# S5 products sent one by one inside the projection tiles of a two-layer trunk

## The chip, the core and the metric

The kernel runs on one core of one Trainium2 chip. Its engines are TensorE (PE in the profile, with its weight loads on a row of their own, PEld), VectorE (DVE), ScalarE (ACT), GpSimd (POOL) and SyncE (SP); the last two mostly issue DMAs here. The metric is the device time of one execution in microseconds (us). "Before" is the kernel without the change, "after" the one with it.

## The reference

```python
for l in range(DEPTH):                                  # DEPTH = 2, SEQ = 256, D_MODEL = 2048
    h = rmsnorm(x, g_pre_mix[l]) * (1.0 + sc1) + sh1
    y = hybrid_mixer(h, positions, w_in[l], w_out[l], ...)
    x = x + gt1 * rmsnorm(y, g_post_mix[l])
    h = rmsnorm(x, g_pre_ffn[l]) * (1.0 + sc2) + sh2
    y = conv_ffn(h, f_w_up[l], f_conv_w[l], f_conv_b[l], f_w_down[l])
    x = x + gt2 * rmsnorm(y, g_post_ffn[l])
...
def hybrid_mixer(...):
    proj = (h @ w_in)
    m_qk, m_v, m_o, m_i, m_f, s_u, n_q, n_kv, n_g = split(proj)
    y_m = mlstm_group(...)                              # 4 heads
    y_s = s5_group(s_u, ...)                            # 32 groups of 16 channels, 64 complex states each
    y_n = nsa_group(...)                                # 8 query heads, attention in "items"
    return concatenate([y_m, y_s, y_n]) @ w_out
...
def s5_group(u, ...):
    x = u @ B                                           # complex: real and imaginary part
    h[t] = a * h[t-1] + x[t]                            # scan over the sequence
    y = gelu(real(C @ h) + d_skip * u)
    return y * sigmoid(y @ w_glu + b_glu)
```

## The kernel before, in words

Everything is float32; a weight chunk of the big products is split into a high part (w_hi, by ScalarE, L1427) and a rest (w_lo, by VectorE, L2015), and TensorE adds three products. The stage of the change is the input projection of each layer: 41 column tiles n = 0 to 40 of 128 columns. A tile (`proj`, L789) takes two weight chunks, one for each half of the 2048 rows; a half is 8 row tiles of 3 matmuls of 256 columns (L798), so a tile is 48 matmuls. In layer 0 the first 12 tiles are made elsewhere, so the loop starts at n = 12.

Between the tiles TensorE gets the other work of the mixer, placed by tile number. For S5 these are blocks of 8 matmuls of 64 (or 63) columns: four input blocks (`s5_in`, L973, h = 0, 1 and part = real, imaginary) behind the tiles 18 to 21, and six output blocks (`s5_out`, L988 and L991) behind the tiles 22, 23, 24, 25, 26 and 26 (`OUT_AT`). Before its first matmul a block waits for its weight chunk (`raw_full`); the first input block also for the S5 tokens, the blocks of h = 1 for VectorE's read of the blocks of h = 0 (`s5_bv`), output blocks with part 1 for the end of the scan (`s5_h`). The last matmul of a block gives the chunk's place free (`raw_used`).

All weight chunks, of 512 KB each, go through one ring of five places in SBUF, in an order fixed beforehand (`_ring_places`): S5's chunk for tile n stands behind the second chunk of tile n+1. SyncE issues the loads in that order and waits at each until the chunk five places earlier has been split (`raw_free`, from VectorE) or used (`raw_used`, from TensorE). S5's own chunks were written to DRAM earlier in the same layer (s_in_w, s_own_w, s_out_w). A split part has four places, so ScalarE may split chunk c+4 once TensorE has used chunk c (`w_used`).

ScalarE and VectorE also work through fixed lists, tile by tile. ScalarE at tile n: split the first chunk of tile n+2 (`w_head(2n+4)`), evict tile n (`in_tile`; L1598 to L1600, L1586), split the second chunk, then the rest of that tile's work. Part of it is `s5_gelu(h)` (16 activations, L1713), which stands at the tile `OUT_AT[3h+2]` and waits for the last output block of h. From tile 27 on (`ITEM_TILE`) attention items run: at n = 27 ScalarE copies the transposed values (L1859) and then does `exps(0)` (L1724); TensorE's `scores(1)`, behind tile 28, waits for the end of `exps(0)` (`ns_e`). VectorE at tile n: `w_rest(2n+4)`, `w_rest(2n+5)` (L2015, w_lo), then for n = 19 to 24 a third of the S5 scan, then slices of the conditioning product (ada, L2021).

```python
CMP_TILE, IN_TILE, OUT_TILE, GLU_TILE, MB_TILE = 10, 18, 22, 32, 35
OUT_AT = [OUT_TILE + i for i in (0, 1, 2, 3, 4, 4)]
...
def scores(n):
    if n: ns_e.wait(pe, l, n)
```

Of the kernel before, what the change touches and what calls it, by code (L numbers as in the profile page):

```python
# [24 lines left out]
P = 128  # L25
# [8 lines left out]
UT = S_GROUPS * S_GROUP // P  # L34
# [3 lines left out]
SN = SEQ // SL  # L38
SH = ST // 2
# [20 lines left out]
KH = KT // 2  # L60
# [50 lines left out]
R_CMP, R_IN, R_OUT, R_GLU = 0, N_CMP, N_CMP + 4, N_CMP + 10  # L111
NRAW = R_GLU + 2
CMP_TILE, IN_TILE, OUT_TILE, GLU_TILE, MB_TILE = 10, 18, 22, 32, 35
OUT_AT = [OUT_TILE + i for i in (0, 1, 2, 3, 4, 4)]
BLOCKS_AT = (HT, CMP_TILE - 3)
CMP_AT = ([HT + 2 + i // 2 for i in range(N_CMP)], [CMP_TILE + i for i in range(N_CMP)])

# [88 lines left out]
def trunk(nc, x, c_cols, pos, consts, aux_d, ada_d, ada_b, glu_d, stream, out):  # L206
    with ExitStack() as ctx:
# [7 lines left out]
        at = nc.sbuf_base - 2 * KT * SEQ * 4  # L215
# [51 lines left out]
        ps = ctx.enter_context(nc.psum_tensor("ps", [P, 8, 512], F32))  # L267
# [32 lines left out]
        def sem(name):  # L300
# [8 lines left out]
        w_used = sem("w_used")  # L309
# [19 lines left out]
        raw_used = Signal("raw_used", NRAW)  # L329
# [24 lines left out]
        s5_u, s5_ut = Signal("s5_u", 1), sem("s5_ut")  # L354
# [3 lines left out]
        s5_tr, s5_tr_ev = Signal("s5_tr", UT), Signal("s5_tr_ev", UT)  # L358
# [3 lines left out]
        s5_bv, s5_h, s5_g = Signal("s5_bv", 2), Signal("s5_h", 2), Signal("s5_g", 2)  # L362
# [6 lines left out]
        ch_g, cc_mm, cc_ev = Signal("ch_g", 2), Signal("cc_mm", 1), Signal("cc_ev", 2)  # L369
# [23 lines left out]
        s5_u2, s5_cos, s5_sin, s5_dec = (  # L393
            S5T[:, 4 * i:4 * i + 4, :].rearrange("p a b -> p (a b)").rearrange("p (j n) -> p j n", j=ST) for i in range(4))
# [25 lines left out]
        s5_v = [[pair(t) for t in (28, 30, 32, 34)], [pair(t) for t in (36, 38, 0, 2)]]  # L420
# [62 lines left out]
        def raw(l, n):  # L483
            if l == 0 and n < CMP_HELD:
                return held((W_S5 + 4, W_S5 + 8, W_S5 + 12, KT // 2, 3 * KT // 4)[n])
            return ring[:, RING_RAW[l][n] % RING, :]
# [252 lines left out]
        def _(pe):  # L739
            def raw_full(l, n):  # L740

                if l == 0 and n < CMP_HELD:
                    pe.wait_ge(cmp_full, 16 * CMP_HELD)
                    return
                pe.wait_ge(ring_full[RING_RAW[l][n] % RING], ring_count(l, RING_RAW[l][n]))
# [40 lines left out]
                m.then_inc(w_used, 2)  # L786
                h_lo.wait(pe, l, 8 * n + 8)

            def proj(l, c, bank):  # L789

                for half in range(2):
                    split_ready(l * NS + c + half)
                    s = (c + half) % SPLIT
                    for kk in range(KH):
                        k = half * KH + kk
                        ks = slice(kk * P, (kk + 1) * P)
                        for p, (w, h) in enumerate(((w_hi, hT_hi), (w_hi, hT_lo), (w_lo, hT_hi))):
                            m = pe.matmul(ps[:, bank, 0:SEQ], w[:, s, ks], h[:, k, :],  # L798
                                          start=k == 0 and p == 0, stop=k == KT - 1 and p == 2)
                    m.then_inc(w_used, 1)  # L800

            def to_tokens(n, x0, c, k, summed=None):

# [75 lines left out]
            for l in range(DEPTH):  # L879
# [80 lines left out]
                                              u[:, :, :, SL - 1 - k], start=True, stop=True)  # L960
                    m.then_inc(s5_ut, 1)

                def s5_in(h, part):

                    n = R_IN + 2 * h + part
                    raw_full(l, n)
                    if h == 0 and part == 0:
                        s5_tr_ev.wait(pe, l, UT)
                        s5_u.wait(pe, l, 1)
                    if h == 1:  # L970
                        s5_bv.wait(pe, l, 1)
                    for j in range(SH):
                        m = pe.matmul(ps[:, 2 + part, j * SN:(j + 1) * SN], raw(l, n)[:, j * P:(j + 1) * P],  # L973
                                      s5_u2[:, SH * h + j, :], start=True, stop=True)
                    raw_used.by(m)

                def s5_out(h, part):

                    n = R_OUT + 3 * h + part
                    raw_full(l, n)  # L980
                    if part == 1:
                        s5_h.wait(pe, l, h + 1)
                    if h == 0 and part == 0:
                        ch_g.wait(pe, l, 2)
                    for j in range(SH):
                        js = slice(j * P, (j + 1) * P)
                        if part == 0:
                            m = pe.matmul(ps[:, 6 - h, j * SN:(j + 1) * SN], raw(l, n)[:, js], s5_u2[:, SH * h + j, :],  # L988
                                          start=j == 0, stop=False)
                        else:  # L990
                            m = pe.matmul(ps[:, 6 - h, j * SN + 1:(j + 1) * SN], raw(l, n)[:, js],  # L991
                                          s5_v[h][part - 1][:, j * SN:(j + 1) * SN - 1], start=False,
                                          stop=part == 2 and j == SH - 1)
                    raw_used.by(m)

                def compress(i):

# [160 lines left out]
                for n in range(0 if l else HT, NT):  # L1158
                    if l == 0 and n < HT + 2:
                        in_ev.wait(pe, l, 2 * (n - HT) + 2)  # L1160
                        h_lo.wait(pe, l, 8)
                    elif n >= 2:
                        if N_QK <= n - 2 < N_V:
                            qk_cv.wait(pe, l, n - 2 - N_QK + 1)
                        else:
                            in_ev.wait(pe, l, n - 1)
                    if n == 0:
                        first_tiles(l, 0, 0)
                    elif n >= 2:
                        proj(l, 2 * n, n % 2)  # L1170
                    if l and n == 1:
                        s5_b_transposes()
                    if l and n - 2 in S5_B:
                        s5_in_weights(S5_B.index(n - 2))
                    if l and n - 3 in S5_B:
                        s5_own_weights(S5_B.index(n - 3))
                    if l == 0 and n == HT + 1:
                        s5_tokens()
                    if l == 0 and n - 3 in LATE_C:
                        s5_own_weights(len(HEAD_OWN) + LATE_C.index(n - 3))  # L1180
                    for i in range(N_CMP):
                        if n == CMP_AT[l][i] + 1 and i % 4 == 3:
                            compress_sum(i // 4)
                    for i in range(N_CMP):
                        if n == CMP_AT[l][i]:
                            compress(i)
                    if n == N_G + 2:
                        gate_columns()
                    if IN_TILE <= n < IN_TILE + 4:
                        s5_in(*divmod(n - IN_TILE, 2))  # L1190
                    if n == CMP_TILE + N_CMP + 2:
                        compressed()
                    for i in range(6):
                        if n == OUT_AT[i]:
                            s5_out(*divmod(i, 3))
                    if n == ITEM_TILE - 2:
                        v_tokens(0)
                    if n == ITEM_TILE:
                        v_tokens(1)
                    if 0 <= n - ITEM_TILE < NI:  # L1200
                        scores(n - ITEM_TILE)
                    if 0 <= n - ITEM_TILE - 1 < NI:
                        weights_t(n - ITEM_TILE - 1)
                    if 0 <= n - ITEM_TILE - 2 < NI:
                        weighted_sum(n - ITEM_TILE - 2)
                    if GLU_TILE <= n < GLU_TILE + 2:
                        glu(n - GLU_TILE)
                    if n == MB_TILE:
                        glu_z.wait(pe, l, 4)
                        gate_turned(0)  # L1210
                        mg_d.wait(pe, l, 2)
                        for ck in range(2):
                            pe.transpose(ps[:, 7, 4 * ck:4 * ck + 4], rows(3, ck * P, (ck + 1) * P), K("ident", 0, 4, 4))
                        m_row.wait(pe, l, 1)
                        for ck in range(2):
                            m = pe.transpose(ps[:, 7, 8 + 4 * ck:12 + 4 * ck], rows(0, ck * P, (ck + 1) * P), K("ident", 0, 4, 4))
                        mb_mm.by(m)
                    if n == NT - 2:
                        select(2, 6, 0)
                    if n == NT - 1:  # L1220
                        mc_a.wait(pe, l, 2)
                        ns_e.wait(pe, l, NI)
                        m_scores(3, 0)
                        m_s.by(m_last[0])
                    if n == NT - 3:
                        m_tokens(0)
                    if n == NT - 2:
                        m_tokens(1)
# [1641 lines left out]
```

## Time and profile before

| | us |
|---|---|
| median of 3 runs (2419.27 to 2421.63) | 2420.58 |
| the profiled execution | 2424.17 |
| its span, from the first to the last instruction | 2422.3 |
| PE busy in the span | 2352.5 (97%) |
| DVE busy | 1860.4 (77%) |
| ACT busy | 1287.5 (53%) |
| mean granted TensorE clock | 0.993 |

Shares of busy time are means over stages with different limits. The projection of layer 0 lies at about 148 to 420 us of the span, that of layer 1 at about 1310 to 1571 us, and S5's blocks at 204 to 275 us and 1387 to 1454 us. In timeline rows the columns are start, length, engine, line, operation, out<-in, shapes and count; lengths of matmuls are modelled ends, so what a matmul costs is read from one start to the next. One float32 matmul of S5 has two records of PE in the profile, so a block of 8 is x16; a matmul of the tiles has one.

### The profile page before, as it was taken

The page shows a single profiled execution, that of the slowest core. Times are in us where ns is not written, and L with a number is a line of the kernel's source. Part 1 is how long each engine was busy: PE and PEld are TensorE (multiplying, and loading weights), DVE is VectorE, ACT ScalarE, POOL GpSimd, SP SyncE. Part 2 cuts the span into 40 slices and gives each one's busy share as a digit, 9 for nine tenths or more (in the row PEclk, how much of TensorE's full clock was granted, in tenths as well). Part 3 has the DMA queues.
Part 4 walks back from the last instruction along what each step waited for, and adds up shares of the span by engine and source line. Part 5 has one row for each costly group of instructions (what it writes and reads, how often), then busy time and mean ns, then how long its engine had stood idle before and what let it go on. Part 6 is the DMA issues. An engine that isn't in the chain of part 4 may idle for free.

```text
span 2422.3 us, 40088 instructions
## 1 busy us (share of the span) xinstructions
PE 2352.5 (97%) x13932; PEld 2057.1 (85%) x13932; DVE 1860.4 (77%) x2739; ACT 1287.5 (53%) x2164; POOL 227.5 (9%) x384
## 2 busy tenths in 40 slices
PE   6899999999999999999999999999999999999998
PEld 5689988788888888888889999887888888888887
DVE  7989998879999999666679987567896666565555
ACT  5365755555455545444468657655555445554444
POOL 1111111101111111000001130000110000000000
PEclk9999999999999999999999999999999999999999
DMA  9999878859999999687756865447795555556554
GB/s 379 401 392 325 288 280 303 307 191 354 333 349 346 343 343 338 244 290 275 271 210 221 295 240 197 162 182 268 284 331 193 189 190 188 186 189 199 201 192 146
DMA packets 189211, 643.06 MB, mean 265 GB/s; under 512 B 19089, under 2 KB 41809, under 8 KB 183329
## 3 DMA queue, kind: packets, MB, share of 16 engines
q1 hardware_dynamic: 125346, 421.72, 48.0%
q0 software_dynamic: 51264, 205.04, 23.9%
q10 hardware_dynamic: 12480, 14.72, 1.7%
q8 instruction: 73, 1.20, 0.2%
q14 instruction: 48, 0.39, 0.1%
HBM read 626.68 MB, written 14.71 MB: 265 GB/s over the span
## 4 chain that ended last, share of the span: by engine, by line
PE 77%; DVE 14%; DMA 5%; ACT 2%; issue 2%; POOL 0%; ACTq 0%; DVEq 0%; POOLq 0%; SPq 0%
PE ps L1346 25%; PE ps L815 18%; PE ps L1354 13%; PE ps L798 8%; PE ps L1243 4%; DVE w_lo L2015 3%; DVE ada_w L2021 3%; DVE mix L2015 2%; DMA ada_w<-ada_d 2%; PE ps L783 2%; DMA ada_lo<-ada_d 1%; PE ps L1257 1%; ACT w_hi L1427 1%; DVE side L2015 1%; DMA ring<-stream 1%
## 5 line engine op out<-in xcount | busy, mean ns | idle before, releaser
L2015 DVE TENSOR_TENSOR w_lo<-ring,w_hi 128x1024 fp32r<-128x1024 f32 x708 | 868.4, 1232 | 427.3 <-ACT w_hi L1427 423.4
L1427 ACT ACTIVATE w_hi<-ring 128x1024 fp32r<-128x1024 f32 x708 | 748.7, 1058 | 787.1 <-PE ps L815 245.2
L1346 PE MATMUL ps<-hT,w_hi 128*128 128x512 f32 x2688 | 642.2, 391 | 0.0
L1346 PEld LDWEIGHTS ps<-hT,w_hi 128*128 128x128 f32 x2688 | 493.8, 188 | 95.8
L2021 DVE SCALAR_TENSOR_TENSOR ada_w<-ada_w,cs_row 128x1024 f32<-128x1024 f32 (+1 forms) x332 | 406.6, 1258 | 16.2 <-DMA ada_w<-ada_d 15.9
L798 PE MATMUL ps<-hT,w_hi 128*128 128x256 f32 x2176 | 407.5, 289 | 5.0 <-DVE w_lo L2015 2.9
L798 PEld LDWEIGHTS ps<-hT,w_hi 128*128 128x128 f32 x2176 | 343.4, 194 | 15.3 <-issue 12.7
L1354 PEld LDWEIGHTS ps<-hT,w_lo 128*128 128x128 f32 x2688 | 344.6, 191 | 13.1
L1354 PE MATMUL ps<-hT,w_lo 128*128 128x256 f32 x2688 | 348.7, 283 | 0.0
L798 PE MATMUL ps<-hT,w_lo 128*128 128x256 f32 x1088 | 309.7, 285 | 0.0
L798 PEld LDWEIGHTS ps<-hT,w_lo 128*128 128x128 f32 x1088 | 210.6, 194 | 0.0
L815 PE MATMUL ps<-w_hi,x_hi 128*128 128x512 f32 x656 | 202.0, 389 | 1.8 <-DVE x_lo L2015 1.8
L815 PE MATMUL ps<-w_hi,x_lo 128*128 128x512 f32 x656 | 202.0, 389 | 0.0
L815 PE MATMUL ps<-w_lo,x_hi 128*128 128x512 f32 x656 | 202.0, 389 | 0.0
L677 POOL DMA_DIRECT2D ada_w<-ada_d x192 | 101.3, 528 | 755.1 <-DVE ada_w L2021 751.4
L815 PEld LDWEIGHTS ps<-w_hi,x_hi 128*128 128x128 f32 x656 | 123.0, 188 | 28.1 <-DVE x_lo L2015 2.7
L815 PEld LDWEIGHTS ps<-w_hi,x_lo 128*128 128x128 f32 x656 | 123.1, 188 | 25.7
L815 PEld LDWEIGHTS ps<-w_lo,x_hi 128*128 128x128 f32 x656 | 123.1, 188 | 25.5
L712 POOL DMA_DIRECT2D ada_w<-ada_d x128 | 68.1, 532 | 627.5 <-DVE ada_w L2021 624.7
L1957 ACT ACTIVATE mix<-ff_a,aux 128x256 f32 (+1 forms) x86 | 51.1, 595 | 90.7 <-DVE ff_a L2015 90.7
L2021 DVE SCALAR_TENSOR_TENSOR mix<-ff_a,aux,mix 128x255 f32 (+3 forms) x172 | 82.9, 482 | 15.8 <-DVE mix L2021 12.2
L872 PE MATMUL ps<-mix,ring 128*128 128x256 f32 x240 | 58.0, 399 | 12.2 <-ACT hT L1569 8.4
(327 smaller groups left out, 2361.2 us busy)
## 6 DMA issues: line engine op xcount, KB each, us to landing
ring<-stream SPq DMA_DIRECT2D x746, 512.0 KB, 4.8
ada_w<-ada_d POOLq DMA_DIRECT2D x320, 512.0 KB, 6.5
ada_w<-ada_d POOLq DMA_DIRECT2D x12, 1024.0 KB, 12.4
ada_lo<-ada_d POOLq DMA_DIRECT2D x10, 1024.0 KB, 15.5
ada_hi<-ada_d POOLq DMA_DIRECT2D x10, 1024.0 KB, 11.9
mix<-stream SPq DMA_DIRECT2D x14, 512.0 KB, 14.5
xs<-x SPq DMA_DIRECT2D x2, 2048.0 KB, 11.1
s_in_w<-mix ACTq DMA_DIRECT2D x8, 512.0 KB, 6.7
```

The costliest lines, as they stand in the source:

```text
L677: pool.dma_start(ada_w[:, s, :], ada_src(u * UG + j // 2, j % 2)).then_inc(ada_full[s], 16)
L712: pool.dma_start(ada_w[:, j % ASLOT, :], ada_src(u * UG + j % ACH // 2, j % 2)).then_inc(ada_full[j % ASLOT], 16)
L798: m = pe.matmul(ps[:, bank, 0:SEQ], w[:, s, ks], h[:, k, :], start=k == 0 and p == 0, stop=k == KT - 1 and p == 2)
L815: m = pe.matmul(ps[:, 4 * t + 2 * half + b, :], xx[:, xs_, ts_], w[:, s, b * 512:(b + 1) * 512], start=k == 0 and p == 0, stop=False)
L872: m = pe.matmul(ps[:, bank, off:off + SEQ], head_w(c)[:, o:o + P], h_f[:, k % HF, :], start=k == 0 and j % 2 == 0, stop=k == KT - 1 and j ...
L1243: m = pe.matmul(ps[:, 4 * t + 2 * half + b, :], xx[:, ts_], w[:, c % SPLIT, b * 512:(b + 1) * 512], start=j % KT == 0 and p == 0, stop=j = ...
L1346: m = pe.matmul(ps[:, bank, :], w_hi[:, (c + half) % SPLIT, kk * P:(kk + 1) * P], hT[:, k, :, :], start=k == 0, stop=k == KT - 1)
L1354: m = pe.matmul(ps[:, bank, SEQ:2 * SEQ], w_lo[:, (c + half) % SPLIT, kk * P:(kk + 1) * P], hT_hi[:, k, :], start=False, stop=False)
L1427: s.activation(w_hi[:, c % SPLIT, :], ring[:, at % RING, :], ACT.Copy).then_inc(hi_ready, 1)
L1957: s.activation(mtile(t), ff_a[:, k % 2, :], ACT.Identity, scale=w, bias=b).then_inc(ff_tap, 1)
L2015: return v.tensor_tensor(o, a, b, op)
L2021: return v.scalar_tensor_tensor(o, a, s, b, op0, op1, accum_out=total)
```

## The change

The S5 products no longer form blocks. `proj` gets a function that it calls behind each row tile, and that sends one product j (0 to 7) of an S5 block there, so that the block's 8 products lie behind the 8 row tiles of one half of a tile. Input blocks: second half of tile 18, second half of 19, first half of 21, second half of 21. Output blocks: second half of the tiles 22 to 27. The block's waits stand before its first product (j = 0), `raw_used` at its last. `OUT_AT` now ends in 27, which moves the sixth output block, its chunk's place in the ring and `s5_gelu(1)` a tile later. `w_used` is raised by the last matmul of the tile's half, ahead of the last S5 product.

```diff
-OUT_AT = [OUT_TILE + i for i in (0, 1, 2, 3, 4, 4)]
+OUT_AT = [OUT_TILE + i for i in range(6)]
+IN_HALF = ((IN_TILE, 1), (IN_TILE + 1, 1), (IN_TILE + 3, 0), (IN_TILE + 3, 1))
...
-            def proj(l, c, bank):
+            def proj(l, c, bank, beside=None):
...
-                    m.then_inc(w_used, 1)
+                        if kk == KH - 1:
+                            m.then_inc(w_used, 1)
+                        if beside:
+                            beside(half, kk)
...
+                def s5_beside(n, half, j):
+
+                    for i, at in enumerate(IN_HALF):
+                        if at == (n, half):
+                            s5_in(*divmod(i, 2), j)
+                    if half == 1 and n in OUT_AT:
+                        s5_out(*divmod(OUT_AT.index(n), 3), j)
...
-                        proj(l, 2 * n, n % 2)
+                        proj(l, 2 * n, n % 2, lambda half, j: s5_beside(n, half, j))
...
-                    if IN_TILE <= n < IN_TILE + 4:
-                        s5_in(*divmod(n - IN_TILE, 2))
...
-                    for i in range(6):
-                        if n == OUT_AT[i]:
-                            s5_out(*divmod(i, 3))
```

Two places show what moves. TensorE in layer 0, end of tile 18, before (L798 the tile, L1014 the sum of the compressed blocks, L1086 the gate columns, L973 the first input block):

```order
L798 MATMUL ps<-hT,w_lo 128x256
L1014 MATMUL ps<-fold,cmp_s 128x30 [waits ch_p]
L1086 MATMUL ps<-cst,sg_59 128x24 [waits in_ev]
L1086 MATMUL ps<-cst,sg_59 128x24
L973 MATMUL ps<-mix,ring 128x64 [waits s5_u,s5_tr_ev,ring_full3]
L973 MATMUL ps<-mix,ring 128x64 x7
L798 MATMUL ps<-hT,w_hi 128x256 [waits raw_free,in_ev]
```

And after, from the start of tile 18's second half (L799 the tile, L977 the input block; the two other groups follow behind the tile):

```order
L799 MATMUL ps<-hT,w_hi 128x256 [waits raw_free]
L799 MATMUL ps<-hT,w_hi 128x256
L799 MATMUL ps<-hT,w_lo 128x256
L977 MATMUL ps<-mix,ring 128x64 [waits s5_u,s5_tr_ev,ring_full3]
L799 MATMUL ps<-hT,w_hi 128x256 x2
L799 MATMUL ps<-hT,w_lo 128x256
L977 MATMUL ps<-mix,ring 128x64
```

The wait for the S5 chunk moved from behind the tile and the two small groups to behind the first row tile of the tile's second half, with 21 matmuls of the tile queued behind it.

ScalarE, tiles 26 and 27, before (L1427 splits, L1586 evictions, L1713 `s5_gelu(1)`, L1859 the copy, L1724 `exps(0)`):

```order
L1586 ACTIVATE mix<-ps,aux 128x256 [waits w_used]
L1427 ACTIVATE w_hi<-ring 128x1024 [waits w_used,ring_full0]
L1713 ACTIVATE mix<-ps 32x128 [waits raw_used]
L1713 ACTIVATE mix<-ps 32x128 x15
L1427 ACTIVATE w_hi<-ring 128x1024 [waits w_used,ring_full1]
L1586 ACTIVATE mix<-ps,aux 128x256 [waits w_used]
L1427 ACTIVATE w_hi<-ring 128x1024 [waits w_used,ring_full2]
L1859 ACTIVATE mix<-ps 128x512 [waits s5_h,vt_mm]
L1724 ACT_TABLE_LOAD
L1724 ACTIVATE side,att_s<-side,att_s 128x15 [waits ns_m]
```

And after (L1436 splits, L1595 evictions, L1722 `s5_gelu(1)`, L1868 the copy, L1733 `exps(0)`):

```order
L1595 ACTIVATE mix<-ps,aux 128x256 [waits w_used]
L1436 ACTIVATE w_hi<-ring 128x1024 [waits w_used,ring_full4]
L1436 ACTIVATE w_hi<-ring 128x1024 [waits w_used,ring_full1]
L1595 ACTIVATE mix<-ps,aux 128x256 [waits w_used]
L1436 ACTIVATE w_hi<-ring 128x1024 [waits w_used,ring_full2]
L1722 ACTIVATE mix<-ps 32x128 [waits raw_used]
L1722 ACTIVATE mix<-ps 32x128 x15
L1868 ACTIVATE mix<-ps 128x512 [waits s5_h,vt_mm]
L1733 ACT_TABLE_LOAD
L1733 ACTIVATE side,att_s<-side,att_s 128x15 [waits ns_m]
```

The 16 activations of `s5_gelu(1)` moved from between the evictions of the tiles 26 and 27 to behind that of tile 27, directly ahead of the copy and `exps(0)`. The lists of VectorE and GpSimd are the same in both kernels.

## Rows read from the trace of the kernel before

**Rows 1.** Chain that ended last, 180 to 460 us: start, us, what
```profile
206.46 7.32 PE ps L798 x48
...
214.97 0.96 ACT w_hi L1427
...
217.09 0.69 DVE mix L2015
...
260.33 1.15 DVE w_lo L2015
261.55 7.92 DMA ring<-s_out_w
269.51 5.25 PE ps L991 x32
274.76 7.48 PE ps L798 x48
```

**Rows 2.** Busy time by stretch: us, PE, PEld, DVE, ACT, POOL, clock, DMA, GB/s
```profile
216.00:262.00 46.00, 45.53 (x386) 45.04 (x384) 45.18 (x60) 19.66 (x36) 4.75 (x9) 1.00 0.82 285
...
1460.00:1545.00 85.00, 85.00 (x628) 77.34 (x627) 55.39 (x104) 60.33 (x137) 2.64 (x5) 1.00 0.51 180
```

**Rows 3.** TensorE's timeline around the second input block, layer 0
```profile
213.60 1.90 PE L973 MATMUL ps<-mix,ring 128*128 128x64 f32 x16
...
215.63 0.28 PE L798 MATMUL ps<-hT,w_lo 128*128 128x256 f32 x1
```

**Rows 4.** TensorE's timeline, products of 128 columns and of 1 in turn
```profile
418.80 0.47 PE L1279 MATMUL ps<-side,mix 128*128 128x128 f32 x2
419.10 0.28 PE L1280 MATMUL ps<-cst,mix 128*128 128x1 f32 x2
419.25 0.47 PE L1279 MATMUL ps<-side,mix 128*128 128x128 f32 x2
```

**Rows 5.** TensorE's timeline, layer 0, second half of tile 18 to tile 19
```profile
199.96 0.40 PE L798 MATMUL ps<-hT,w_hi 128*128 128x256 f32 x2
...
200.32 0.40 PE L798 MATMUL ps<-hT,w_hi 128*128 128x256 f32 x2
...
203.90 0.41 PE L1014 MATMUL ps<-fold,cmp_s 128*128 128x30 f32 x2 [0.90 <-ACT cmp_s L1759]
...
206.27 0.48 PE L798 MATMUL ps<-hT,w_hi 128*128 128x256 f32 x2
```

**Rows 6.** SyncE's timeline: the load of the first input block's chunk
```profile
194.49 0.61 SPq L588 DMA_DIRECT2D ring<-s_in_w  x1
```

**Rows 7.** DMA view of that load alone: KB, us to landing
```profile
ring<-s_in_w SPq DMA_DIRECT2D x1, 512.0 KB, 8.3
```

**Rows 8.** Busy time by stretch, layer 0, columns as in rows 2
```profile
268.20:271.60 3.40, 2.42 (x21) 2.22 (x21) 3.33 (x6) 0.00 (x0) 0.53 (x1) 1.00 0.78 252
271.60:275.00 3.40, 3.40 (x18) 3.40 (x18) 3.37 (x7) 1.51 (x2) 0.00 (x0) 0.50 0.94 348
...
278.40:281.80 3.40, 3.40 (x30) 3.40 (x30) 3.40 (x7) 3.31 (x9) 1.03 (x2) 0.99 1.01 383
```

**Rows 9.** ScalarE's timeline, layer 1, tiles 26 and 27
```profile
1454.39 6.53 ACT L1713 ACTIVATE mix<-ps 32x128 f32<-32x128 f32 x16 [2.01 <-PE ps L991]
...
1462.03 0.56 ACT L1586 ACTIVATE mix<-ps,aux 128x256 f32<-128x256 f32 x1
...
1463.44 0.59 ACT L1859 ACTIVATE mix<-ps 128x512 f32<-128x512 f32 x1
...
1466.52 1.04 ACT L1427 ACTIVATE w_hi<-ring 128x1024 fp32r<-128x1024 f32 x1
```

**Rows 10.** TensorE's timeline, layer 1: end of tile 27, end of tile 28
```profile
1460.00 0.60 PE L1034 MATMUL ps<-cst,mix 128*128 128x128 f32 x4
...
1467.09 0.61 PE L1106 MATMUL ps<-mix 128*128 128x128 f32 x4
```

**Rows 11.** VectorE's timeline, layer 1: start of the S5 scan
```profile
1401.09 2.87 DVE L2015 TENSOR_TENSOR mix<-ps,mix 128x512 f32<-128x512 f32 x4 [1.59 <-DMA s_out_w<-mix]
```

**Rows 12.** TensorE's timeline, layer 1: third input block and the next tile
```profile
1404.10 1.97 PE L973 MATMUL ps<-mix,ring 128*128 128x64 f32 x16 [1.06 <-DVE mix L2015]
...
1406.73 0.50 PE L798 MATMUL ps<-hT,w_hi 128*128 128x256 f32 x2
```

More of the change, by code:

```diff
@@ L961, in s5_tokens, with s5_in @@
                     m.then_inc(s5_ut, 1)
-                def s5_in(h, part):
+                def s5_in(h, part, j):
                     n = R_IN + 2 * h + part
[L966 to L975, printed above, removed]
@@ L977, in s5_out @@
-                def s5_out(h, part):
-                    n = R_OUT + 3 * h + part
[L980 to L994, printed above, removed]
+                    if j == 0:
+                        raw_full(l, n)
+                        if h == 0 and part == 0:
+                            s5_tr_ev.wait(pe, l, UT)
+                            s5_u.wait(pe, l, 1)
+                        if h == 1:
+                            s5_bv.wait(pe, l, 1)
@@ new lines, in s5_in, with s5_out @@
+                    m = pe.matmul(ps[:, 2 + part, j * SN:(j + 1) * SN], raw(l, n)[:, j * P:(j + 1) * P],
+                                  s5_u2[:, SH * h + j, :], start=True, stop=True)
+                    if j == SH - 1:
+                        raw_used.by(m)
+                def s5_out(h, part, j):
+                    n = R_OUT + 3 * h + part
+                    if j == 0:
+                        raw_full(l, n)
+                        if part == 1:
+                            s5_h.wait(pe, l, h + 1)
+                        if h == 0 and part == 0:
+                            ch_g.wait(pe, l, 2)
+                    js = slice(j * P, (j + 1) * P)
+                    if part == 0:
+                        m = pe.matmul(ps[:, 6 - h, j * SN:(j + 1) * SN], raw(l, n)[:, js], s5_u2[:, SH * h + j, :],
+                                      start=j == 0, stop=False)
+                    else:
+                        m = pe.matmul(ps[:, 6 - h, j * SN + 1:(j + 1) * SN], raw(l, n)[:, js],
+                                      s5_v[h][part - 1][:, j * SN:(j + 1) * SN - 1], start=False,
+                                      stop=part == 2 and j == SH - 1)
+                    if j == SH - 1:
+                        raw_used.by(m)
```

## The prediction

> **What bounds the kernel now.** I read the chain that ended last first, then busy time by stretch, then the timelines of single engines around each place that the change touches. In layer 0 the chain runs from tile 19 on TensorE over one split on ScalarE to VectorE, stays on VectorE from 217.09 to 261.48 us, goes through the load of an S5 output chunk and comes back to TensorE at 269.51 [rows 1]. VectorE is busy 45.18 of the 46 us there, and TensorE 45.53 [rows 2]: both are full, so a delay of either stays. In layer 1 TensorE alone is full (85.00 of 85.00 us against 55.39 on VectorE) [rows 2]. What TensorE loses in layer 1 is therefore lost, and in layer 0 what the end of tile 19 loses is handed to VectorE.
>
> **The products themselves: no gain.** A block of 8 runs from 213.60 to the third matmul of the next tile at 215.63, and two of the tile's matmuls in it are worth 0.24 (three take 0.36 [rows 5]), so a block costs 2.03 - 0.24 = 1.79 us, 0.224 for a product and 0.112 for each of its two records [rows 3]. The hope of the edit would be that a product's weight loads hide behind the wide matmuls around it. Against that: where pairs with 128 columns and pairs with 1 column alternate, four records take 419.25 - 418.80 = 0.45, again 0.112 each, however narrow the matmul [rows 4]. So the time goes by weight loads, one per record, and a wide matmul (0.12) leaves only 0.008 above its own. The first load of a product hides behind the wide matmul ahead of it, the second load and the load of the wide matmul behind it stand open: 2 x 0.112, the 0.224 of the block. 20 blocks x 8 = 160 products then cost what they did, 35.8 us in all. Bounds: if one of the two loads vanished, -160 x 0.112 = -17.9 us; if a third load stood open at each product, the one that the wide matmul ahead now hides, +17.9. I take 0, since rows 4 are the nearest thing to the new order.
>
> The Trainium skill, page "TensorE: Matmul & The Clock Gate", section "LDWEIGHTS (loading the stationary operand)", makes a load's time go by its weight columns alone, about 107 ns for 128; the 0.112 of the rows agrees. The same page's section on the array's detail says that TensorE's queue can pull weight loads ahead of matmuls in flight; by that rule the loads could vanish as in the second rival. Rows 4 do not show it.
>
> **Layer 0, tile 18.** The wait for the input chunk moves ahead of 21 matmuls. The second half starts at 199.96, so the first product is due at 200.32 [rows 5]. The load was issued at 194.49 and took 8.3 [rows 6, 7]: it lands at 202.8, and nothing before it changes. TensorE waits 2.5 us. Then 21 x 0.12 + 1.79 = 4.3, so the tile ends at 207.1. The two small groups behind it (before, from 203.90 to 206.27 less the block's 1.79, that is 0.58) bring tile 19 to 207.7, against 206.27: +1.4. Before, TensorE waited 0.90 there for ScalarE's cmp_s [rows 5]; that wait goes, as the tile ends later, and is in the sum.
>
> Tile 19 now holds its block too, so its eviction, and ScalarE's next split behind it in the list, come 1.4 + 1.79 = 3.2 later. VectorE waits for that split and then has no slack to 261.48 [rows 1, 2], and the output chunk behind its last piece lands 3.2 later: 269.51 becomes 272.7. Waits of TensorE for other output chunks on the way are longer too, but all end ahead of this landing. The bill there is smaller than before: two blocks in a row took 269.51 to 274.76, 5.25 us, at the low clock [rows 1, 8]; after the landing there now come 21 x 0.12 + 1.79 = 4.3 to the end of tile 26 (277.0) and 48 x 0.12 + 1.79 = 7.55 to the end of tile 27: 284.6, against 274.76 + 7.48 = 282.2. So +2.4 in layer 0 by the end of tile 27. The clock: a stretch with TensorE busy 2.42 of 3.40 was followed by one granted 0.50 (1.2 GHz instead of 2.4), with 18 records where 30 fit at full clock [rows 8]. In 3.4 us at 0.12 there fit 28, so such a stretch costs 10 x 0.12 = 1.2. Two go (behind the double block) and one or two come (behind the new waits), ahead of a landing that VectorE sets; I count 0, bounds -1.2 and +1.2.
>
> **Both layers, tile 27: the step that costs most.** `s5_gelu(1)` now stands ahead of `exps(0)` on ScalarE, and needs the end of tile 27. Before, it filled a hole in which ScalarE waited 2.01 us for TensorE [rows 9]. Layer 1, from the end of tile 27: eviction and split 1463.44 - 1462.03 = 1.41, now gelu 6.53, then copy, table load and exps(0) 1466.52 - 1463.44 = 3.08: 11.0 us [rows 9]. TensorE comes to `scores(1)` 1467.09 - 1460.00 = 7.09 after the end of tile 27 [rows 10] and waits for `exps(0)`: 3.9, and about 4.0 with the eviction's start behind the tile. Before, `exps(0)` was done at 1466.52, 0.57 ahead of need [rows 9, 10]. The lists are the same in layer 0, so 4.0 there too; VectorE's `weighted(0)` also waits for `exps(0)`, so its full list shifts with it and gives nothing back. Queued behind: tile 29's products on TensorE, slices of ada on VectorE. Bounds 3.5 and 4.5. A hole of 4 us leaves at least one stretch of 3.4 with less TensorE work than the 2.42 above, so the low clock follows: +1.2 in layer 1, where TensorE is the bound; in layer 0 VectorE's list hides about half: +0.6.
>
> **Layer 1, tile 18 to 21.** All chunks land early there. But ScalarE issues the last S5 weights' stores while it evicts tile 18, which ends 1.79 later; VectorE's scan waited 1.59 us for them, to 1401.09 [rows 11], and now starts at 1402.9; TensorE's third block, released at 1404.10 [rows 12], is released at 1405.9. From there 16 products and 45 matmuls of tile 21 are left: 3.58 + 5.40, end 1414.9. Before: 1406.73 [rows 12] + 5.76 + 1.79 = 1414.3. So +0.6, bounds -1.2 (the wait hidden) and +1.5.
>
> **Edits with one answer.** The sixth chunk's place in the ring moves two loads back, and tile 28's two chunks come forward; each can land a tile ahead of its use on TensorE. The third input chunk is given free a half tile and a block later (2.88 + 1.79, less the block that tile 20 no longer has ahead: some 3 us) and holds SyncE's queue so long; the split behind it waits for TensorE's tile 21 anyway. Counted 0; if it delayed VectorE as tile 19 does, at most +1.
>
> **Sum.** Layer 0: 2.4 + 4.0 + 0.6 = 7.0. Layer 1: 0.6 + 4.0 + 1.2 = 5.8. Together +12.8, so the profiled execution's 2424.17 (span 2422.3) would be 2437.0. It lies 3.6 above the median of the runs; on the median 2420.58 the forecast is 2433.4. Its own bounds, +8 to +18, give 2428 to 2439.
>
> **Rivals.** *The queues absorb it.* If ScalarE ran `exps(0)` in time and the scan's stores were not on the path, 4.0 x 2, 1.8 of clock and 0.6 go and layer 0's +2.4 stays: 2423. For it: such holes are often filled elsewhere; against it: both lists are fixed and rows 9 and 10 leave 0.57.
> *Hidden loads, the other side.* If a product's second load vanished behind the wide matmuls, the sum would be 12.8 - 17.9 = -5.1: 2415.5. It decides from 0.08 us saved for each product. Against it: rows 4, and VectorE's bound in layer 0.
> *Costlier switches.* With a third load open at each product: 2433.4 + 17.9 = 2451. Against it: the 2.03 of rows 3 are 16 records and two wide matmuls to the hundredth, so the switches of a block cost nothing.
> *More low clock.* If each new wait (layer 0: tiles 18, 24, 26, 28; layer 1: 21, 28) costs a further stretch: +6 x 1.2 = 7, 2440.
> *The products do not move as told:* the two pieces of the order shown above say that they do; no chance.
>
> **Chances.** Forecast 0.70, absorbed 0.10, hidden loads 0.07, costlier switches 0.04, more low clock 0.09. About 0.2% (4.8 us) is what a measurement of this kernel can tell from no change. Faster by more: 0.06 (hidden loads, save a little that ends within). Within: 0.11 (absorbed and that rest). Slower: 0.83. The range 2425 to 2440 takes the forecast with its bounds and most of the low-clock case; it leaves out hidden loads, most of the absorbed case and costlier switches, under 0.2.
>
> **What would show it.** In the profile after: a wait of TensorE for the S5 chunk of about 2.5 us near 200 to 203 us; TensorE waits of about 4 us behind tile 28 in both layers, put down to ScalarE's L1733, and the clock at 0.50 after them; matmuls of L799 and L977 at 0.12 and 0.224 as before; the wait for the scan near 1404 us at about 1.7 instead of 1.06. I am wrong if a tile with S5 in it takes less than 7.4 us where nothing waits (hidden loads), or if `exps(0)` ends ahead of tile 28 (absorbed).

## The result, and the profile after

After takes 2435.06 us in the median (2429.08 to 2440.44) against 2420.39 before on the same chip: a ratio of 1.006, 95% interval 1.0041 to 1.0079, so 10 to 19 us slower. The forecast was 2433.4, with 83% for slower by over 0.2%. The profiled execution of after took 2440.44 us, a span of 2438.7, 16.3 more than the profiled one of before; its mean granted clock is 0.990 against 0.993. The six executions of after lie in two groups, 2429.08 to 2431.65 and 2438.47 to 2440.44: none is near the median, the profiled one is the longest, and what parts the groups is not known, since only that one has a trace.

TensorE's waits come first, since TensorE is full in both layers. This is the view of waits of after, layer 0 from 195 to 330 us (line waited at, releaser: us in total, times, longest):

```profile
PE ps L996 <- DMA ring<-s_out_w: 4.1, 2, 3.6
PE ps L1120 <- ACT side L1733: 3.9, 1, 3.9
PE ps L977 <- DMA ring<-s_in_w: 2.0, 1, 2.0
```

The same view, layer 1 from 1385 to 1580 us:

```profile
PE ps L1120 <- ACT side L1733: 3.9, 1, 3.9
PE ps L977 <- DVE mix L2024: 2.0, 1, 2.0
```

The two rows of 3.9 are `scores(1)` behind `exps(0)`; before has no such wait in either layer. ScalarE's timeline of after shows why, in layer 1, tiles 27 and 28 (start, length, then as in [rows 9]; L1595 eviction, L1722 `s5_gelu(1)`, L1733 `exps(0)`, L1436 the split behind it):

```profile
1469.92 0.56 ACT L1595 ACTIVATE mix<-ps,aux 128x256 f32<-128x256 f32 x1 [3.31 <-PE ps L799]
...
1471.33 6.47 ACT L1722 ACTIVATE mix<-ps 32x128 f32<-32x128 f32 x16
...
1478.44 1.28 ACT L1733 ACT_TABLE_LOAD   x1
...
1480.91 1.04 ACT L1436 ACTIVATE w_hi<-ring 128x1024 fp32r<-128x1024 f32 x1
```

From the eviction to the end of `exps(0)` it is 1480.91 - 1469.92 = 11.0 us, as forecast; before, gelu stood ahead of the eviction of tile 27 and the rest took 1466.52 - 1462.03 = 4.5 [rows 9]. ScalarE waits 3.31 us ahead of the eviction and cannot start gelu there. TensorE's timeline of after, the end of tile 28, `scores(1)` and the first matmuls of tile 29:

```profile
1476.85 0.28 PE L799 MATMUL ps<-hT,w_lo 128*128 128x256 f32 x1
1481.05 1.22 PE L1120 MATMUL ps<-mix 128*128 128x128 f32 x4 [3.92 <-ACT side L1733]
...
1484.06 0.78 PE L799 MATMUL ps<-hT,w_hi 128*128 128x256 f32 x2
1484.63 0.41 PE L799 MATMUL ps<-hT,w_lo 128*128 128x256 f32 x1
1484.84 0.63 PE L799 MATMUL ps<-hT,w_hi 128*128 128x256 f32 x2
```

Before, scores(1)'s four records took 0.61 [rows 10]; here 1.22, and the matmuls of tile 29 come every 0.21 and not every 0.12: the clock is low. Busy time by stretch of after says for how long (columns as in [rows 2]; granted clock behind POOL's):

```profile
1475.50:1478.90 3.40, 1.63 (x14) 1.43 (x12) 0.00 (x0) 3.30 (x8) 0.00 (x0) 1.00 1.02 400
1478.90:1482.30 3.40, 1.25 (x6) 1.19 (x7) 0.79 (x4) 3.39 (x11) 0.00 (x0) 0.52 0.39 159
1482.30:1485.70 3.40, 3.40 (x18) 3.08 (x17) 2.11 (x3) 2.30 (x8) 0.00 (x0) 0.50 0.00 0
```

Two stretches are granted 0.52 and 0.50 (1.2 GHz), the first of them while TensorE still waits; the forecast counted one. In the stretch ahead of them TensorE is busy 1.63 of 3.40, and in the first of them 1.25.

The products themselves cost what they did. TensorE's timeline of after, layer 1, tile 19, one row tile and the next:

```profile
1395.01 0.33 PE L977 MATMUL ps<-mix,ring 128*128 128x64 f32 x2
1395.15 0.48 PE L799 MATMUL ps<-hT,w_hi 128*128 128x256 f32 x2
1395.47 0.29 PE L799 MATMUL ps<-hT,w_lo 128*128 128x256 f32 x1
1395.60 0.33 PE L977 MATMUL ps<-mix,ring 128*128 128x64 f32 x2
```

From product to product it is 1395.60 - 1395.01 = 0.59: three matmuls of the tile at 0.12 and 0.23 for the product, against 0.224 in a block [rows 3].

In layer 0 the wait for the first input chunk has come, as rows of TensorE's timeline of after show (the second half of tile 18, shown for before in [rows 5], and the starts of the tiles 19 and 20):

```profile
202.43 0.28 PE L799 MATMUL ps<-hT,w_lo 128*128 128x256 f32 x1
204.68 0.43 PE L977 MATMUL ps<-mix,ring 128*128 128x64 f32 x2 [1.98 <-DMA ring<-s_in_w]
...
211.08 0.50 PE L799 MATMUL ps<-hT,w_hi 128*128 128x256 f32 x2
...
218.62 0.48 PE L799 MATMUL ps<-hT,w_hi 128*128 128x256 f32 x2
```

And the chain that ended last of after runs over both waits for chunks and then over ScalarE (start, us, what; [rows 1] are those of before):

```profile
196.71 7.93 DMA ring<-s_in_w
...
249.68 7.82 DMA ring<-s_out_w
...
296.30 1.28 ACT L1733
...
298.92 1.23 PE ps L1120 x4
```

The output chunk behind VectorE's stretch of the chain is now that of tile 24, where before it was that of the block behind tile 26 [rows 1]. TensorE waits 3.58 of the 4.1 us above for it, and at the tiles 26 and 27 it does not wait (its timeline, second half of tile 24):

```profile
257.54 0.69 PE L996 MATMUL ps<-mix,ring 128*128 128x63 f32 x2 [3.58 <-DMA ring<-s_out_w]
```

How far each profiled execution has fallen behind that of before is the table on which the rest stands (us, worked out from starts and ends in TensorE's timelines; T18 is the start of tile 18, T27e the end of tile 27, L0 and L1 the layers). TensorE has the same work behind it in all rows, but for two things: in x2_last_block_later a block of 1.79 us is still to come at L0 T27e, and x7_filler and x10_filler_short have extra matmuls in the wait ahead of T30.

| | L0 T18 | L0 T22 | L0 T27e | L0 T28e | L0 T30 | L0 T33 | L1 T18 | L1 T28e | L1 T30 | end |
|---|---|---|---|---|---|---|---|---|---|---|
| after | 2.2 | 3.2 | 5.5 | 5.7 | 12.4 | 10.5 | 9.4 | 9.9 | 16.3 | 16.3 |
| x9_gelu_only | 0.5 | 0.4 | 0.4 | 0.4 | 7.0 | 5.3 | 2.1 | 6.6 | 13.5 | 13.5 |
| x1_blocks_in_tile | 0.3 | -1.5 | -0.5 | -0.5 | 6.1 | 4.4 | 2.1 | 1.7 | 8.8 | 8.7 |
| x2_last_block_later | 1.2 | 1.1 | -2.7 | -1.0 | 2.3 | 2.3 | -0.7 | -2.1 | 0.9 | 0.9 |
| x3_two_in_tile26 | 0.5 | -1.8 | 6.0 | 6.0 | 6.0 | 6.0 | 3.2 | 9.0 | 9.7 | 9.7 |
| x4_gelu_behind_exps | 0.4 | -2.4 | -0.4 | -0.2 | 6.2 | 5.6 | 3.7 | 7.5 | 13.1 | 14.9 |
| x5_first_in_19 | 1.5 | 0.4 | 1.9 | 2.1 | 8.5 | 6.8 | 4.7 | 3.5 | 9.3 | 9.4 |
| x7_filler | 1.3 | 0.4 | 2.5 | 2.6 | 9.8 | 9.3 | 8.7 | 7.0 | 14.4 | 14.4 |
| x10_filler_short | 0.7 | 3.8 | 4.6 | 4.8 | 9.2 | 9.3 | 7.5 | 5.8 | 10.0 | 10.9 |
| x8_third_in_only | 1.3 | 0.1 | -0.5 | -0.5 | 0.9 | 0.9 | -0.5 | -1.9 | -1.9 | -1.9 |

The column L0 T18 lies ahead of every edit, so 0.3 to 2.2 us there is how much two executions differ anyway. Between L0 T33 and L1 T18, where nothing was edited, every row falls, by 0.6 to 3.2: there the execution of before was the long one.

### The profile page after: what moved, and what is told of

It reads as the page before. It is cut to its first block, busy times and chain, and to the rows that moved or that the text cites. A ratio compares the mean times of both kernels' runs of the same rounds, so it can differ in the third digit from the quotient of the medians.

```text
span 2438.7 us, 40088 instructions
## 1 busy us (share of the span) xinstructions
PE 2359.9 (97%) x13932; PEld 2063.0 (85%) x13932; DVE 1862.4 (76%) x2739; ACT 1288.4 (53%) x2164; POOL 227.6 (9%) x384
## 4 chain that ended last, share of the span: by engine, by line
PE 74%; DVE 14%; DMA 6%; ACT 4%; issue 3%; POOL 0%; ACTq 0%; DVEq 0%; POOLq 0%; SPq 0%
PE ps L1355 22%; PE ps L819 18%; PE ps L1363 12%; PE ps L799 9%; PE ps L1252 4%; DVE w_lo L2024 3%; DVE ada_w L2030 3%; DMA ada_w<-ada_d 2%; DVE mix L2024 2%; PE ps L784 2%; DMA ada_lo<-ada_d 1%; ACT w_hi L1436 1%; PE ps L1266 1%; DVE side L2024 1%; PE ps L1120 1%
## 5 line engine op out<-in xcount | busy, mean ns | idle before, releaser
L1436 ACT ACTIVATE w_hi<-ring 128x1024 fp32r<-128x1024 f32 x708 | 749.0, 1058 | 779.9 <-PE ps L819 245.2
L799 PE MATMUL ps<-hT,w_hi 128*128 128x256 f32 x2176 | 426.4, 295 | 6.5 <-DVE w_lo L2024 4.4
L799 PEld LDWEIGHTS ps<-hT,w_hi 128*128 128x128 f32 x2176 | 343.4, 194 | 17.0 <-issue 14.4
L799 PE MATMUL ps<-hT,w_lo 128*128 128x256 f32 x1088 | 310.1, 285 | 0.0
L799 PEld LDWEIGHTS ps<-hT,w_lo 128*128 128x128 f32 x1088 | 210.6, 194 | 0.0
## 6 DMA issues: line engine op xcount, KB each, us to landing
ada_w<-ada_d POOLq DMA_DIRECT2D x12, 1024.0 KB, 12.4
mix<-stream SPq DMA_DIRECT2D x14, 512.0 KB, 12.8
```

The lines of the kernel that those rows point to most:

```text
L799: m = pe.matmul(ps[:, bank, 0:SEQ], w[:, s, ks], h[:, k, :], start=k == 0 and p == 0, stop=k == KT - 1 and p == 2)
L1436: s.activation(w_hi[:, c % SPLIT, :], ring[:, at % RING, :], ACT.Copy).then_inc(hi_ready, 1)
```

## The experiments

Medians are in us, with the ratio to the kernel before on the same chip and its 95% interval. Each expectation explains the theories that it names.

### The places kept, the products again in blocks

x1_blocks_in_tile is after with a block's 8 products sent together behind the first row tile of its half.

```diff
+                    if j:
+                        return
...
-                            s5_in(*divmod(i, 2), j)
+                            for jj in range(SH):
+                                s5_in(*divmod(i, 2), jj)
...
-                        s5_out(*divmod(OUT_AT.index(n), 3), j)
+                        for jj in range(SH):
+                            s5_out(*divmod(OUT_AT.index(n), 3), jj)
```

> The change with one thing undone: the 8 products of a block stand together again, behind the first row tile of the same half tile; waits, releases, chunk places and s5_gelu(1) stay where the change put them. Theory Q (the cost lies in what waits moved past): the time of the changed kernel, 2429 to 2440, with waits of 3.9 to 4.2 us for exps(0) in both layers and a block at 1.79 us, as products cost 0.224 either way. Rival P (sending products one by one costs in itself, about 14 us over 160 products): back to about 2421.

Measured: 2437.81, ratio 1.0087 (1.0063 to 1.0112), no faster than after. The waits of TensorE, layer 0; the last row reads the same in layer 1:

```profile
PE ps L996 <- DMA ring<-s_out_w: 3.4, 2, 3.1
PE ps L977 <- DMA ring<-s_in_w: 0.7, 1, 0.7
...
PE ps L1124 <- ACT side L1737: 4.1, 1, 4.1
```

So sending the products one by one is not what costs; the places are, that of `s5_gelu(1)` among them.

### The slot alone, all in blocks behind their tiles

x2_last_block_later is before with the sixth output block behind tile 27, and with it `s5_gelu(1)`.

```diff
-OUT_AT = [OUT_TILE + i for i in (0, 1, 2, 3, 4, 4)]
+OUT_AT = [OUT_TILE + i for i in range(6)]
```

> The kernel before with one thing done: only the sixth output block, its chunk's place and s5_gelu(1) move from tile 26 to tile 27, all in blocks. Theory Q: s5_gelu(1) now waits for the block behind tile 27; exps(0) ends 1.79 + 6.53 + 3.08 = 11.4 after the tile, TensorE needs it 1.79 + 7.09 = 8.9 after it, so a wait of about 2.5 us in each layer, low clock behind it (1.2 to 2.4 each), less 1 to 3 us in layer 0 where the double block goes: 2424 to 2429. Rival P: 2420, since no product is sent alone.

Measured: 2425.81, ratio 1.002 (1.001 to 1.0029). The waits of TensorE, layer 0; the last row reads the same in layer 1:

```profile
PE ps L991 <- DMA ring<-s_out_w: 1.3, 1, 1.3
...
PE ps L1106 <- ACT side L1724: 2.7, 1, 2.7
```

The wait for `exps(0)` is 1.2 shorter than in after, since the block itself (1.79) keeps TensorE busy behind tile 27 while ScalarE evicts. Two things are cheaper here. Layer 0 gains 2.2 up to the end of tile 28 (table: -1.0 against +1.2 at tile 18): no double block is left, and from 271.60 to 278.40 us the two stretches of 3.40 are granted 0.60 and 0.90, where before has 0.50 in both. That the edit did this is not shown, since x8_third_in_only keeps the double block and has 0.90 and 0.60 there. And behind the wait of 2.7 the clock stayed up, as busy time by stretch shows in layer 1, though TensorE is busy only 0.69 of 3.40 in the first row:

```profile
1464.50:1467.90 3.40, 0.69 (x7) 0.49 (x5) 0.03 (x1) 3.35 (x12) 0.00 (x0) 1.00 0.67 254
1467.90:1471.30 3.40, 3.40 (x29) 3.32 (x30) 2.75 (x7) 3.40 (x9) 0.00 (x0) 1.00 0.01 6
```

### One by one, the slot undone

x3_two_in_tile26 is after with the fifth and the sixth block's products both in the second half of tile 26, and `s5_gelu(1)` back at tile 26.

```diff
-OUT_AT = [OUT_TILE + i for i in range(6)]
+OUT_AT = [OUT_TILE + i for i in (0, 1, 2, 3, 4, 4)]
...
-                    if half == 1 and n in OUT_AT:
-                        s5_out(*divmod(OUT_AT.index(n), 3), j)
+                    for i, at in enumerate(OUT_AT):
+                        if half == 1 and at == n:
+                            s5_out(*divmod(i, 3), j)
```

> The change with the other thing undone: products one by one everywhere, but the fifth and the sixth output block both lie behind the row tiles of tile 26's second half, and the sixth chunk's place and s5_gelu(1) are back at tile 26. Theory Q: no wait for exps(0) in either layer; what stays is tile 18's wait and its hand-over in layer 0 (about 2.4 to 3) and 0.6 in layer 1: 2422 to 2426. Rival P: 2431 to 2435, since all 160 products are still sent one by one.

Measured: 2425.9, ratio 1.0023 (1.0012 to 1.0033): 9 us less than after. The waits of TensorE, layer 0 (the first row) and layer 1:

```profile
PE ps L996 <- DMA ring<-s_out_w: 4.9, 4, 2.5
...
PE ps L977 <- DVE mix L2025: 3.6, 1, 3.6
...
PE ps L1121 <- ACT side L1734: 0.5, 1, 0.5
```

No wait of 4 us for `exps(0)` is left. The profiled execution took 2433.85, 8 us over the median. Its loss from tile 22 to the end of 27 (+7.8, the waits for output chunks and a clock of 0.50 from 271.2 to 284.8 us) and at the scan (+5.7 from tile 18 to the end of 28 in layer 1) is therefore likely above what this kernel mostly pays, and where the median's 5.8 us lie is not settled.

### The gelu behind exps(0)

x4_gelu_behind_exps is after with `s5_gelu(1)` behind `exps(0)` on ScalarE.

```diff
-                        if n == OUT_AT[3 * h + 2]:
+                        if h == 0 and n == OUT_AT[3 * h + 2]:
                             s5_gelu(h)
...
                         exps(n - ITEM_TILE)
+                    if n == ITEM_TILE:
+                        s5_gelu(1)
```

> The change with s5_gelu(1) behind exps(0) on ScalarE, still at tile 27. Theory Q, if the order of these two is all: no wait behind tile 28, about 2425. Theory R (ScalarE has no room of 6.5 us among the items, wherever it stands): exps(0) is in time, but exps(1) comes 6.5 us of gelu and one or two table loads of 1.28 later, TensorE waits 3 to 4 us for it behind tile 29 instead, and the time stays at 2431 to 2438.

Measured: 2435.44, ratio 1.0059 (1.0042 to 1.0076), the time of after. The wait is the same, a tile later: TensorE's timeline, layer 1, behind tile 29:

```profile
1485.81 0.71 PE L1120 MATMUL ps<-mix 128*128 128x128 f32 x4 [3.78 <-ACT side L1733]
```

ScalarE has no room for 6.5 us in either of these two places; the hole ahead of tile 27's eviction, where before had the gelu, has it. Other places were not tried.

### The gelu alone moved

x9_gelu_only does to the kernel before one thing: `s5_gelu(1)` a tile later. All products stay where they were.

```diff
-                        if n == OUT_AT[3 * h + 2]:
+                        if n == OUT_AT[3 * h + 2] + h:
```

> The kernel before with one edit: s5_gelu(1) stands one tile later on ScalarE, at tile 27 ahead of the copy and exps(0). All products stay in their blocks, the double block behind tile 26 included. Theory R (the loss is ScalarE's list): TensorE waits about 3.9 us for exps(0) behind tile 28 in each layer, s_out_w waits as before, and with two stretches at the low clock behind each wait the time is 8 to 12 above before, 2428 to 2432. Rival Q (the loss is in where the products stand): at most 2 above before, under 2422.5.

Measured: 2435.34, ratio 1.0045 (1.0029 to 1.006), so 7 to 15 us slower; the median is 3 above the 2428 to 2432 of Theory R. The waits of TensorE, layer 1; the first row reads the same in layer 0:

```profile
PE ps L1106 <- ACT side L1724: 4.1, 1, 4.1
PE ps L973 <- DVE mix L2015: 2.5, 1, 2.5
```

This is the largest part of after's loss, made without moving a product. From the end of tile 28 to tile 30 it loses 6.6 in layer 0 and 6.9 in layer 1, after 6.8 and 6.4. The L973 row is another thing: nothing near it was changed, yet the wait for the scan was 2.5 and not 1.06 [rows 12], and cost 4.5 (table, L1 T18 to T28e), since the clock was low behind it, as busy time by stretch shows:

```profile
1409.70:1413.10 3.40, 3.40 (x16) 2.80 (x17) 3.40 (x4) 0.45 (x2) 2.34 (x3) 0.50 0.46 141
```

### The wait filled with matmuls

x7_filler puts 17 extra matmuls ahead of the wait in after, x10_filler_short 9; their result is not used.

```diff
+                    if n == 1:
+                        for i in range(17):
+                            pe.matmul(ps[:, 7, 0:SEQ], ident, cst[:, 0:SEQ], start=True, stop=True)
                     if n:
                         ns_e.wait(pe, l, n)
```

> The kernel after, with 17 extra matmuls of 256 columns (34 records, about 3.8 us) in an unused bank ahead of TensorE's wait for exps(0) in each layer; their result is not used. They fill the wait without shortening it, so ScalarE ends exps(0) when it did. If the low clock behind the wait costs 2.4 us in each layer, as two stretches at half speed say, the time is 3 to 5 below after, 2430 to 2432, with no granted clock of 0.50 behind tile 28. If the low clock costs what the forecast said (1.2 and 0.6), 1 to 2 below after, 2433 to 2434. If it costs nothing, 2435 or more.

> The kernel after with 9 extra matmuls (18 records) ahead of TensorE's wait for exps(0) in each layer, result not used. In the run with 17 of them a record took 7.33 / 34 = 0.216 us, so 18 take 3.88 us, about the wait itself, and ScalarE's exps(0) comes when it did. If the two stretches at the low clock behind the wait cost what layer 1's trace of after says (6.43 lost from the end of tile 28 to tile 30, less a wait of 4.08, so 2.35) in layer 1 and half of it in layer 0, the time is 3 to 4 below after, 2431 to 2432, with the clock at 1.00 behind tile 28 and the loss from the end of tile 28 to tile 30 at 4.0 to 4.3 in layer 1. If the low clock costs nothing of its own, 2434 or more.

Measured: 2437.95, ratio 1.0065 (1.0049 to 1.008), with 17; 2434.49, ratio 1.0058 (1.0041 to 1.0075), with 9. The first was mis-sized. I took 0.112 a record, which holds for narrow matmuls; with 256 columns of plain float32 it is twice that, as TensorE's timeline of x7_filler shows in layer 1:

```profile
1474.12 7.50 PE L1107 MATMUL ps<-cst 128*128 128x256 f32 x34
1481.46 0.61 PE L1123 MATMUL ps<-mix 128*128 128x128 f32 x4
```

7.34 us of filler overran the wait by 3.4. With 9 it fits, and the clock is granted in full; busy time by stretch of x10_filler_short, layer 1, from `scores(1)` on:

```profile
1476.50:1479.90 3.40, 3.35 (x27) 2.87 (x27) 2.32 (x6) 3.40 (x10) 0.00 (x0) 1.00 0.00 0
1479.90:1483.30 3.40, 3.40 (x31) 3.40 (x30) 3.33 (x6) 3.34 (x12) 0.00 (x0) 1.00 0.47 151
```

From the end of tile 28 to tile 30 of layer 1 it now loses 10.0 - 5.8 = 4.2, where after lost 6.4: the low clock behind the wait costs 2.2 there. In layer 0 the same difference, 2.3 at tile 30, has shrunk to 10.51 - 5.65 - (9.25 - 4.75) = 0.36 by tile 33 (the table's numbers with one more digit). I had expected the whole time to be 3 to 4 below after. It is 0.6 below, in the expectation's other range (2434 or more, if the low clock costs nothing of its own), while the 4.2 of layer 1 is in the first (4.0 to 4.3). The two intervals lie over each other, so the times neither confirm nor exclude the 2.2 us of layer 1 and the 0.4 of layer 0 that the traces show.

### The first input block later

x5_first_in_19 gives the first input block the first half of tile 19.

```diff
-IN_HALF = ((IN_TILE, 1), (IN_TILE + 1, 1), (IN_TILE + 3, 0), (IN_TILE + 3, 1))
+IN_HALF = ((IN_TILE + 1, 0), (IN_TILE + 1, 1), (IN_TILE + 3, 0), (IN_TILE + 3, 1))
```

> The kernel after, with the first input block behind the row tiles of tile 19's first half instead of tile 18's second half, so that its chunk is due 4 us later. The forecast's layer 0 term said that the 2.5 us wait at tile 18 is handed on to the end of the S5 scan. If that is so, the wait goes and the end of tile 27 comes up to 2.5 us earlier: 2432.5 to 2434. Rival: what sets the end of tile 27 is the wait for the fifth chunk's landing at tile 24, which VectorE sets by the scan; then layer 0 changes by under 0.7 us and the time stays at 2434.5 to 2436.

Measured: 2431.08, ratio 1.0036 (1.0023 to 1.0049). The waits of TensorE, layer 0:

```profile
PE ps L1120 <- ACT side L1733: 3.9, 1, 3.9
PE ps L996 <- DMA ring<-s_out_w: 3.7, 1, 3.7
```

The wait for the input chunk is gone and the end of tile 27 is 0.4 late against tile 18, where in after it was 3.2, though the wait at tile 24 is as long as ever. So the loss by the end of tile 27 comes from the wait at tile 18, which is handed on, as forecast; the rival that the landing at tile 24 sets it alone does not hold. That it is the wait and not the place, x1_blocks_in_tile and x4_gelu_behind_exps show: their block stands in tile 18, waits 0.7 and not at all, and they lose nothing up to there. The time fell by 4.0 against after, somewhat more than expected; the intervals touch (1.0041 to 1.0049 is in both), and other executions differ by as much.

### The third input block alone

x8_third_in_only is before with one part of the change: the third input block goes one by one into the first half of tile 21. The cut is against after; the lines that put the other blocks back behind their tiles are left out.

```diff
-OUT_AT = [OUT_TILE + i for i in range(6)]
-IN_HALF = ((IN_TILE, 1), (IN_TILE + 1, 1), (IN_TILE + 3, 0), (IN_TILE + 3, 1))
+OUT_AT = [OUT_TILE + i for i in (0, 1, 2, 3, 4, 4)]
+IN_HALF = (None, None, (IN_TILE + 3, 0), None)
...
```

> The kernel before with one part of the change alone: only the third input block's 8 products lie behind the row tiles of tile 21's first half; all others stay in blocks behind their tiles. It was the part that waited for the scan in layer 1 (1.06 us). If one product by itself costs what it does in the block, layer 1 gains up to 1.1 us and layer 0 stays: 2419 to 2420.5. If one-by-one products cost a third load (0.112 each), +1.8 for the two layers less the 1.1: 2421.

Measured: 2419.09 over 11 runs (2417.96 to 2422.6) against 2421.42, ratio 0.999 (0.9981 to 0.9999). It is the one version whose interval lies ahead of both kernels, of before by 0.2 to 4.6 us, so only just. TensorE's timeline, layer 1, the first two products:

```profile
1403.59 0.33 PE L977 MATMUL ps<-mix,ring 128*128 128x64 f32 x2
...
1404.16 0.33 PE L977 MATMUL ps<-mix,ring 128*128 128x64 f32 x2
```

Products at 0.57 a row tile again, and no wait for the scan. That the wait went because of the edit is not shown: in x2_last_block_later, where this block stood as before, it was not there either.

## Why the prediction was right, step by step

- **Products at no gain: right.** At the full clock, 0.57 to 0.59 us a row tile with a product in every kernel that has them, three wide matmuls and 0.21 to 0.23; the first row tile of a half shows 0.50. Tile 19 of layer 0 as a whole took 218.62 - 211.08 = 7.54 in after, against 48 x 0.12 + 1.79 = 7.55, so the sign of hidden loads, under 7.4, did not come. The Trainium skill, page "TensorE: Matmul & The Clock Gate", section on the array's detail, has TensorE's queue pull weight loads ahead of matmuls in flight; by that the second rival would have hidden half of a product. The rows above show no such saving: a product between wide matmuls costs what it does in a block.
- **`s5_gelu(1)` ahead of `exps(0)`: right, and the largest term.** Forecast: 11.0 us on ScalarE against 7.09 on TensorE, a wait of 3.9 in each layer. Measured 11.0 and 3.9 (4.1 where only the gelu moved). x9_gelu_only alone lost 7 to 15 of the 10 to 19; x3_two_in_tile26, without it, was 9 faster than after. The rival "the queues absorb it" fell with these waits; x4_gelu_behind_exps shows that one place further on has no room either.
- **The low clock behind it: mechanism right, size off in layer 1.** The step was "at least one stretch of 3.4 with less TensorE work than the 2.42 above, so the low clock follows: +1.2 in layer 1". Two stretches came, and x10_filler_short puts them at 2.2. In layer 0 the forecast 0.6 was 0.4 by tile 33.
- **Layer 0, tile 18: the hand-over right, the path behind it wrong, the number near by luck.** Forecast: a wait of 2.5, and +2.4 by the end of tile 27, set by the landing of tile 26's chunk, with all other waits ahead of it. After: 2.0 and 3.2 (5.5 less the 2.2 that were there before), but by the 3.58 at tile 24 and a clock of 0.50 from 257.1 to 263.9 us behind it; no wait came at the tiles 26 and 27. x10_filler_short: 2.6 and 3.9. But x7_filler: 1.7 and 1.2; x1_blocks_in_tile: 0.7 and -0.7; x4_gelu_behind_exps: none and -0.8, with the same input block places in all. What varies is the load's time to land (see below); I had taken one row of one execution, 8.3 [rows 7], for its value. The forecast also left out a low clock that before has in tile 19, as busy time by stretch shows:

```profile
206.77:210.18 3.41, 3.41 (x18) 3.41 (x18) 3.26 (x5) 3.38 (x4) 0.00 (x0) 0.50 0.89 344
```

  Tile 19 to tile 20 takes 9.04 us there and 7.54 in after. Where the chunk landed in time (x4_gelu_behind_exps), no low clock came there, and tile 20 starts 2.7 us earlier against tile 18 than in before. Up to the end of tile 28 the clock is at 0.50 for 10.2 us in before (206.8 to 210.2, 271.6 to 278.4) and for 10.2 in after (205.9 to 209.3, 257.1 to 263.9), so the 0 counted for it came out, though three stretches went and three came.
- **Layer 1, tile 18 to 21: right in after, and no property of the change.** Forecast +0.6, after 0.5 to the end of tile 28, with a wait of 2.0 instead of 1.7. But between executions the scan's wait for the stores ran from none to 4.0 us, also where nothing near was changed (x9_gelu_only: +4.5).
- **The sum.** After against before, profiled: 2.2 ahead of the edits, 3.2 by tile 27, 0.2 to the end of tile 28, 4.9 for the wait in layer 0 by tile 33, -1.1 until tile 18 of layer 1, 0.5 there, 6.4 for the wait in layer 1: 16.3, what the two profiled executions are apart. The forecast's four sizes were 2.4, 4.6, 0.6 and 5.2, 12.8 in all; the median moved by 14.7. The two large terms were read off ScalarE's list and stand on several kernels; the two small ones hit what varies, and that 2433.4 lies so near a median between two groups of executions is luck too.

## What to carry to other kernels

A step moved "one slot later" carries its consumers and producers on the other engines with it: look on the engine that does the follow-up work (here 16 activations on ScalarE) for the hole that it filled, and for what is next in that list. Work fitted into ScalarE's forced wait was free there and in neither of the two later places tried, so the move here made a wait of 4 us in each layer though TensorE's own work stayed the same. In layer 1, where TensorE is the bound, waits of 3.9 to 4.1 us for `exps(0)` cost 5.8 to 7.1, the low clock behind them included, and one of 2.7 cost 3.0 with the clock up; but behind the 2.5 for the scan in x9_gelu_only the clock fell, so the length of a wait alone does not tell what it costs.

## What the runs showed of the hardware

**The same load lands at very different times.** The load of the first input chunk, 512 KB, was issued at 194.5 to 196.7 us in the profiled executions of all eleven kernels (KB, us to landing; the DMA view of that load alone, here of x4_gelu_behind_exps, after and x5_first_in_19 in turn; the others lie between):

```profile
ring<-s_in_w SPq DMA_DIRECT2D x1, 512.0 KB, 5.7
...
ring<-s_in_w SPq DMA_DIRECT2D x1, 512.0 KB, 7.9
...
ring<-s_in_w SPq DMA_DIRECT2D x1, 512.0 KB, 9.4
```

From 5.7 to 9.4 us with nothing edited ahead of it. A forecast that sets a DMA's landing against a due time within 2 or 3 us should carry that spread in its range.

**The scan's wait for stores also varies.** VectorE's timeline, layer 1, start of the scan, of x4_gelu_behind_exps and of x8_third_in_only (where no wait is noted):

```profile
1408.48 2.87 DVE L2026 TENSOR_TENSOR mix<-ps,mix 128x512 f32<-128x512 f32 x4 [4.00 <-DMA s_out_w<-mix]
...
1398.64 2.85 DVE L2029 TENSOR_TENSOR mix<-ps,mix 128x512 f32<-128x512 f32 x4
```

**The clock depends on more than the length of a wait.** Behind 3.9 to 4.1 us of waiting in layer 1, after, x1_blocks_in_tile and x9_gelu_only lost 6.4 to 7.1 us from the end of tile 28 to tile 30, and x5_first_in_19 with the same 3.9 lost 5.8. The first three have the clock at 0.50 for 6.8 us, x5_first_in_19 for 3.4. Behind 2.7 us in x2_last_block_later the clock stayed at 1.00, though a stretch with TensorE busy 0.69 of 3.40 lay there, less than the 2.42 that the forecast went by; behind 2.5 us in x9_gelu_only it was at 0.50 for 6.8 us. What decides between these was not tested.

**A plain float32 matmul of 256 columns takes 0.43 us** (7.34 / 17 in x7_filler, at a granted clock of 1.00), 3.6 times the 0.12 of the tiles' matmuls of the same size on their split operands.
